# Three chunks of a modulation product moved from one layer's attention to the next stage's tail

## What is computed

```python
def second_block(x, c, w_ada, b_ada, ...):
    c_act = jax.nn.silu(c)
    for l in range(2):
        mod = c_act @ w_ada[l] + b_ada[l]            # 1024 -> 3072, for each layer
        shift, scale, gate = jnp.split(mod, 3, axis=-1)
        h = rmsnorm_2(x, g_pre[l]) * (1.0 + scale) + shift
        p = h @ w_in[l]                              # split: convolution, gates, query, key/value
        y_conv = conformer_conv(...) * silu(g_conv)  # 31 taps, layernorm, silu, @ w_pw2
        y_attn = dsa_attention(...) * silu(g_attn)
        y = jnp.concatenate([y_conv, y_attn], axis=-1) @ w_out[l]
        x = x + gate * rmsnorm_2(y, g_post[l])
    return x
```

## Time and profile before

| what | us |
|---|---|
| median of 3 runs | 939.52 (938.94 to 939.89) |
| the profiled execution, device time | 938.87 |
| its span, first to last instruction | 937.1 |
| PE busy / DVE busy / ACT busy | 929.0 / 820.2 / 279.2 |

### The profile page before, as it was taken

One profiled execution on the slowest core, in us unless ns is written; L12 is line 12 of the kernel. 1 busy time (PEld: TensorE's weight loads), 2 busy tenths in 40 slices (PEclk: granted clock), 3 DMA queues, 4 the chain that ended last, 5 costly groups with the idle time before them and its releaser, 6 DMA issues.

```text
span 937.1 us, 16357 instructions
## 1 busy us (share of the span) xinstructions
PE 929.0 (99%) x6546; PEld 868.2 (93%) x6546; DVE 820.2 (88%) x1854; ACT 279.2 (30%) x628; POOL 1.4 (0%) x8
## 2 busy tenths in 40 slices
PE   9999999999999999999999999999999999999997
PEld 8889999999999998889999999999898888898886
DVE  5779999999999988779999999998899985899963
ACT  1032122222222011263122221220424563624561
POOL 0000000000000000000000000000000000000000
PEclk9999999999999999999999999999999999999999
DMA  9952555464544750757254555546962428443101
GB/s 351 403 190 81 193 190 203 145 238 168 238 166 146 247 231 9 296 210 286 94 198 170 213 191 214 185 156 215 353 227 95 164 92 285 154 155 106 33 1 46
DMA packets 36573, 171.88 MB, mean 183 GB/s; under 512 B 5000, under 2 KB 8592, under 8 KB 23056
## 3 DMA queue, kind: packets, MB, share of 16 engines
q1 hardware_dynamic: 34976, 168.94, 49.1%
q10 hardware_dynamic: 1520, 1.89, 0.6%
HBM read 169.74 MB, written 2.64 MB: 184 GB/s over the span
## 4 chain that ended last, share of the span: by engine, by line
PE 99%; DMA 0%; DVE 0%; issue 0%; ACT 0%; DVEq 0%
PE bank L1353 29%; PE bank L1425 15%; PE bank L1073 10%; PE bank L1745 6%; PE bank L1511 5%; PE bank L1138 4%; PE bank L1731 3%; PE bank L1331 3%; PE bank L1145 3%; PE bank L1609 2%; PE bank L1628 2%; PE bank L1119 2%; PE bank L1551 1%; PE bank L1085 1%; PE bank L1677 1%; PE bank L1657 1%
## 5 line engine op out<-in xcount | busy, mean ns | idle before, releaser
L1425 PE MATMUL bank<-work,fring 128*128 128x128 f32 x1008 | 115.5, 275 | 0.0
L1425 PEld LDWEIGHTS bank<-work,fring 128*128 128x128 f32 x1008 | 114.0, 192 | 0.0
L2598 DVE SCALAR_TENSOR_TENSOR work<-work,cols 128x256 f32<-128x256 f32 x240 | 98.9, 479 | 1.0 <-ACT work L925 0.5
L1353 PE MATMUL bank<-sq,fring 128*128 128x128 f32 x640 | 84.2, 275 | 0.0
L745 ACT ACTIVATE work<-work,cols 128x256 f32<-128x256 f32 x88 | 48.0, 594 | 104.7 <-DVE work L2326 92.3
L1353 PE MATMUL bank<-ring,fring 128*128 128x128 f32 x640 | 78.0, 275 | 0.0
L1353 PE MATMUL bank<-sq,ring 128*128 128x128 f32 x640 | 78.0, 275 | 0.0
L1353 PEld LDWEIGHTS bank<-sq,fring 128*128 128x128 f32 x640 | 77.7, 192 | 0.0
L1353 PEld LDWEIGHTS bank<-ring,fring 128*128 128x128 f32 x640 | 74.7, 192 | 0.0
L1353 PEld LDWEIGHTS bank<-sq,ring 128*128 128x128 f32 x640 | 74.7, 192 | 0.0
L2339 DVE SCALAR_TENSOR_TENSOR work<-work,cols 128x256 f32<-128x256 f32 x176 | 71.5, 478 | 0.0
(11 more groups left out here) (433 smaller groups left out, 1748.0 us busy)
## 6 DMA issues: line engine op xcount, KB each, us to landing
ring<-in_ring SPq DMA_DIRECT2D x60, 1024.0 KB, 7.0
fring<-in_up SPq DMA_DIRECT2D x44, 1024.0 KB, 7.0
ada_w<-in_ada SPq DMA_DIRECT2D x48, 512.0 KB, 6.4
fring<-in_down SPq DMA_DIRECT2D x44, 512.0 KB, 4.8
ring<-in_ring SPq DMA_DIRECT2D x2, 800.0 KB, 5.7
ring<-in_first SPq DMA_DIRECT2D x3, 512.0 KB, 6.2
bias_skewed<-bias_rows SPq DMA_DIRECT2D x1, 1536.0 KB, 13.9
consts<-in_consts SPq DMA_DIRECT2D x1, 1185.5 KB, 10.0
```

The costliest lines, as they stand in the source:

```text
L1353: last = mm(bank[:, P * at:P * (at + 1)], w[:, k, P * c:P * (c + 1)], x[:, k, :], start=(k == 0), stop=(k == 3))
L1425: last = mm(bank[:, at + P * c:at + P * (c + 1)], w[:, P * c:P * (c + 1)], x, start=(i == 0 and at == 0 and c == 0), stop=(i == FF_STEPS - 1),
L2598: marks[c] = link(v.scalar_tensor_tensor(b_y[:, c, :], b_a[:, c, tap:tap + T], col("conv_w_2", 124 * l + 4 * tap + c), b_y[:, c, :], ALU.m ...
```

## The change

Three of MoBA's six chunks leave the attention: they are taken behind the heads 1 to 3 only. Every later chunk's number at a given place is lower by three through the second FFN (chunks 18 to 33 there in place of 21 to 36), and the three are made up in the tail of layer 0: its groups are 3, 4, 3, 3 and 1 chunks in place of 2, 3, 2, 3 and 1 (chunks 34 to 47). The loads follow: `load_ada(21, 24)` ahead of the ring's slots 32 to 35 is gone, the second FFN's loads count from 18, and the tail loads chunks 37 to 44 in one group in place of 40 to 44. Chunk 47 remains the last.

```diff
@@ the second FFN's loads @@
-                a = (0, 21)[f]
+                a = (0, 18)[f]
@@ SP, between the two FFNs @@
-            load_ada(21, 24)
@@ SP, behind the ring's slots 48 to 50 @@
-                    load_ada(40, 45)
+                    load_ada(37, 45)
@@ DVE, MoBA's attention @@
-... lambda n: ada(1) if 1 <= n < 7 else None)
+... lambda n: ada(1) if 1 <= n < 4 else None)
@@ DVE, tail of layer 0 @@
                 if l == 0:
-                    ada(2)
+                    ada(3)
                 mean_square(logs(l, VAR), pb[3][:, 0:T], ms[:, 0:T], D_CONV)
...
                 if l == 0:
-                    ada(3)
+                    ada(4)
                 dve.wait_ge(S("conv_gate"), l + 1)
...
                         if l == 0:
-                            ada(2)
+                            ada(3)
                         product(dve, n + 11)
```

More of the change, by code:

```diff
@@ L2554, in _ @@
             pair_sums(3)
-            attention(0, A_DH ** -0.5, lambda n: pc("mask_ts", DIAG), lambda n: ada(1) if 1 <= n < 7 else None)
+            attention(0, A_DH ** -0.5, lambda n: pc("mask_ts", DIAG), lambda n: ada(1) if 1 <= n < 4 else None)
             out_weight_terms(1)
```

## The result

| | before | after |
|---|---|---|
| median, us | 939.48 (938.94 to 939.89, 6 runs) | 944.73 (943.31 to 945.91, 6 runs) |
| ratio, 95% interval | | 1.0058 (1.0046 to 1.0070) |
| the profiled execution, device time / span | 938.87 / 937.1 | 944.56 / 942.8 |

The change makes the kernel 5.25 us slower. That is the direction forecast, but 1.9 us above the forecast 942.8 and 0.2 us beyond the end of the range.

A forecast was written before the change was run, and what follows sets the result against it. PE, busy 929.0 of 937.1 us, was taken to bound the kernel. Terms 0 + 0 + 3.25 us of PE's wait took the profiled 938.87 to 942.1 and the median 939.52 to 942.8; range 941.6 to 944.5.

The forecast's parts named there:

- The attention's gain of 0: MoBA's heads: three chunks less free 3.45 us of DVE, but PE has no idle time there, so gain 0.
- The chain of loads: Tail of layer 0: chunks 37, 40, 43, each load waiting for the one before; PE waits 3.25 us inside `mix`.
- Both products late: Rival, tail of layer 0: landings nearer 5.0 us make both products with the gate late; 5.4 us, 944.9, chance 0.07.
- late next: Tail's last groups: chunk 47 done at 793.8, first diagonal by 795.3, PE at L1843 at 795.7; held by 0.4 us.
- 0 + 0 + 3.25: Whole kernel: two terms of 0 and PE's wait of 3.25 us in layer 0's tail; profiled 938.87 becomes 942.1.
- the falling clock: Rival: PE's clock falls in its `mix` wait, so 3.3 us of work behind takes 6.6; 946.1, chance 0.06.
- the landing times: Loads of chunks 40 and 43 in layer 0's tail: 3.5 us each gives 2.45 us of wait, 5.0 each 5.4.
- the case outside it: The clock rival at PE's wait in `mix`: 946.1, chance 0.06, left outside the range 941.6 to 944.5.

The follow-up runs named there:

- the run of MoBA's part alone: Against the kernel after: attention has three chunks less, made nowhere else (45 in all), tail keeps its old groups; 939.03 us, before 939.26, ratio 0.9999.
- the same kernel: Kernel before plus four multiplications nothing needs on DVE ahead of the second product with the gate; 941.65 us, later 942.28 and 942.17.

## Why the prediction was wrong

**What held.** The attention's gain of 0, with the period (3.37) and DVE's idle time (2.06 measured, 2.1 forecast) as named; the run of MoBA's part alone shows it in time. The chain of loads: chunk 40 late by 1.31 us (1.5 forecast), chunk 43 by 0.71 (0.6), and PE's wait 3.28 us for 3.25, at the place and with the releaser named. That the wait agrees within 0.03 us is partly luck: chunk 40 was 0.2 us earlier than forecast, on the clock of the trace before, and chunk 43 landed 4.4 us after its issue, where 4.05 was forecast; over the traces of the kernel after the wait is 3.08 to 3.36. The run without the loads of chunks 40 to 43 gives the split between loads and DVE's work. "Both products late" did not come about: the first was ready in time, PE's `mix` starts without idle time. What was "late next" held as well: no wait of PE before the first L1842, and 0.55 before the second, for 0.54 before.

**The step that failed** is the one that left the clock out of the sum. "0 + 0 + 3.25" has everything behind the wait merely shift, at a clock of 1.00; the falling clock stood beside it as a rival with the chance 0.06 and the price 3.3, outside the range. In all three traces of the kernel after the clock fell, and the second part of `mix` took 13.88 us for 12.08, which adds 1.80 us that the sum had at nothing: 939.48 + 3.28 + 1.80 = 944.56, the median is 944.73.

The chance rested on one row: at the program's end the clock was still full in the microsecond in which PE stopped and was first below it some 5 us later. I read that as how long a rest must be. One fall gives no threshold. The runs show falls after rests of 2.38, 3.08, 3.28, 3.36, 3.51 and 5.65 us and none after 1.27, 1.99 and 2.05. And the fall need not lie in the rest: in the kernel after it came 4.2 us after PE had stopped and 1.0 us after it had work again. The end of the program, the only case at hand, could not show that, for there nothing was left to be slowed.

The Trainium skill ("TensorE: Matmul & The Clock Gate", section "HAM oscillation — how this bites in real kernels") tells a kernel's author to leave TensorE no idle gaps beyond a certain length. The traces don't bear that length out as a safe bound: the clock fell behind rests of 2.38 and 3.08 us, both shorter.

The price was too high. I let the clock be low until 3.3 us of full-speed work had been done. Measured is a stretch of 3.4 us (once 6.8), in which half the work is done; it costs 1.7 (once 2.9), and no more behind a rest of 5.65 us. With chance and price right the forecast would have been 939.5 + 3.25 + 1.8 = 944.6.

**The range** ended at 944.5 and went by the landing times alone; the case outside it was the one that came.

## What to carry to other kernels

Work that is fed through a ring of k slots, each load issued when its slot is freed, can come k at a time. The next one in a group waits for a landing time that starts only when the group's first is done; what the engine has to do meanwhile covers a part of it (here 1.31 us of idle time were left of 3.6). So such a group must not stand ahead of something that the bound engine waits for: moving one of the tail's fourteen chunks behind the product took 3.2 us off a loss of 5.3.

Price a pause of TensorE with the clock behind it. In this kernel all six traces with a pause of 2.38 to 5.65 us show the fall, and five of them lose 1.7 us by it; at 2.05 and 1.99 us the clock held, and one execution without a trace seems to have held it at about 3.5. Where the pause can't be avoided, matmuls that compute nothing may be worth putting there.

Time taken off an engine that waits for the bound one buys nothing, and the same work put where the bound engine waits is paid: here 3.45 us of DVE's work cost 5.25.

## What the runs showed of the hardware that I had not expected

The clock can fall after PE has resumed: full from 784.23 to about 785.2, then half for 3.4 us of dense matmuls. And rests nearly alike can differ: 2.05 and 1.99 us kept the clock, 2.38 us lost it in the same kernel, and that kernel's eighteen executions reach from 940.95 to 943.94 where those of before lie within about 1 us. Which of them depends on the rest's length and which on its moment, these runs do not settle.
